# A two-layer transformer block on one core: the memory gemms and the last input projections are moved into the attention mixer, and the softmax rows are scaled on GpSimd

## The reference, cut to what matters

```python
for l in range(DEPTH):
    h = rmsnorm(x, norm_mix[l])
    proj = h @ w_in[l]
    ua, cq, ckv, kr, qc, kc, vc, ud = jnp.split(proj, IN_SPLITS, axis=-1)
    ya = conformer_conv(ua, ...)      # gate, 31-tap depthwise convolution, layernorm, silu, 256x256
    yb = mla(cq, ckv, kr, ...)        # 4 heads: softmax(q k' * 96**-0.5 + mask) v
    yc = diff_attention(qc, kc, vc, positions, rel_bias, ...)   # softmax(a) - lam * softmax(b), heads of 32
    yd = multiscale_pool(ud, ...)     # windows of 2, 4, 8, 16 tokens
    x = x + jnp.concatenate([ya, yb, yc, yd], axis=-1) @ w_out[l]
    x = x + memory_cross_attention(rmsnorm(x, norm_xa[l]), mem, mem_norm[l],
                                   xa_wq[l], xa_wk[l], xa_wv[l], xa_wo[l])
    x = x + conv_glu_ffn(rmsnorm(x, norm_ffn[l]), ffn_up[l], ffn_dw[l], ffn_dw_b[l], ffn_down[l])
return rmsnorm(x, norm_final)
```

## Time and profile before

| | us |
|---|---|
| median of 3 runs (1737.64 to 1742.45) | 1741.35 |
| the profiled execution, its own time | 1740.95 |
| its span, first to last instruction | 1739.2 |
| TensorE busy in the span | 1626.3 |
| VectorE busy | 1104.0 |
| ScalarE busy | 706.7 |
| GpSimd busy | 235.1 |

### The profile page before, as it was taken

The page is one execution under the profiler, slowest core; times in us unless marked ns, Lnnn a source line. Parts: engine busy times, 40 slices in busy tenths (PEclk is TensorE's granted clock), DMA queues, the critical chain, the costliest instruction groups (busy, mean ns, idle before and its releaser), DMA issues. The chain is left out here.

```text
span 1739.2 us, 22473 instructions
## 1 busy us (share of the span) xinstructions
PE 1626.3 (94%) x7664; PEld 1279.8 (74%) x7664; DVE 1104.0 (63%) x1604; ACT 706.7 (41%) x1082; POOL 235.1 (14%) x212
## 2 busy tenths in 40 slices
PE   6889989889999999999998999988999999999996
PEld 3567687668767888888876768657867788888874
DVE  8967974775445764764764886485444674575575
ACT  3232345763334432432442335674243442342343
POOL 5510511112012000000020150112102000000002
PEclk9889999999999999999998999999999999999998
DMA  3143133322212233323224224241211333332323
GB/s 135 47 155 97 61 121 98 103 67 89 81 36 86 97 95 93 96 94 95 94 86 134 83 73 132 78 129 52 94 49 63 95 97 96 97 96 90 99 80 109
DMA packets 50048, 159.69 MB, mean 92 GB/s; under 512 B 6576, under 2 KB 6832, under 8 KB 49072
## 3 DMA queue, kind: packets, MB, share of 16 engines
q1 hardware_dynamic: 49968, 158.63, 29.4%
HBM read 144.97 MB, written 7.34 MB: 88 GB/s over the span
## 5 line engine op out<-in xcount | busy, mean ns | idle before, releaser
L675 ACT ACTIVATE wh<-raw 128x1024 fp32r<-128x1024 f32 x246 | 260.9, 1061 | 657.5 <-PE psum L1235 646.3
L1233 PE MATMUL psum<-a_hi,wh 128*128 128x512 f32 x1072 | 423.1, 395 | 7.8 <-DVE wl L927 7.2
L927 DVE TENSOR_TENSOR wl<-raw,wh 128x1024 fp32r<-128x1024 f32 x246 | 302.7, 1231 | 189.6 <-ACT wh L675 189.4
L1234 PE MATMUL psum<-a_lo,wh 128*128 128x512 f32 x1072 | 419.6, 391 | 0.0
L1235 PE MATMUL psum<-a_hi,wl 128*128 128x512 f32 x1072 | 419.1, 391 | 0.0
L1233 PE MATMUL psum<-b_hi,wh 128*128 128x512 f32 x608 | 239.7, 394 | 5.6 <-DVE wl L927 2.5
L1233 PEld LDWEIGHTS psum<-a_hi,wh 128*128 128x128 f32 x1072 | 202.6, 189 | 56.8 <-DVE wl L927 12.2
L1234 PE MATMUL psum<-b_lo,wh 128*128 128x512 f32 x608 | 236.7, 389 | 0.0
L1235 PE MATMUL psum<-b_hi,wl 128*128 128x512 f32 x608 | 236.7, 389 | 0.0
L1234 PEld LDWEIGHTS psum<-a_lo,wh 128*128 128x128 f32 x1072 | 202.8, 189 | 43.1 <-issue 1.4
L1235 PEld LDWEIGHTS psum<-a_hi,wl 128*128 128x128 f32 x1072 | 202.7, 189 | 42.7
(11 more groups left out here) (209 smaller groups left out, 2145.3 us busy)
## 6 DMA issues: line engine op xcount, KB each, us to landing
raw<-in_w_main SPq DMA_DIRECT2D x106, 512.0 KB, 3.5
raw<-in_w_up SPq DMA_DIRECT2D x88, 512.0 KB, 3.5
raw<-in_w_down SPq DMA_DIRECT2D x32, 512.0 KB, 3.5
bias<-bias_scratch SPq DMA_DIRECT2D x32, 256.0 KB, 2.9
terms<-qk SPq DMA_DIRECT2D x48, 128.0 KB, 2.5
raw<-in_w_last SPq DMA_DIRECT2D x16, 384.0 KB, 3.0
bias_scratch<-stage SPq DMA_DIRECT2D x64, 64.0 KB, 1.6
raw<-in_w_first SPq DMA_DIRECT2D x6, 512.0 KB, 3.6
```

The lines of the kernel that those rows point to most:

```text
L675: act.activation(wh[:, b].rearrange("p k m -> p (k m)")[:, 0:width], raw[:, b, 0:width], ACT.Copy).then_inc(w_hi, 1)
L927: dve.tensor_tensor(wl[:, b].rearrange("p k m -> p (k m)"), raw[:, b, :], wh[:, b].rearrange("p k m -> p (k m)").bitcast(F32), ALU.subtrac ...
L1233: pe.matmul(out_ap, wh[:, b, k, :], his[:, k, :], start=(begin and i == 0), stop=False)
L1234: pe.matmul(out_ap, wh[:, b, k, :], los[:, k, :], start=False, stop=False)
```

## The change

- Projections 11 to 14, the eight memory key gemms and the eight memory value gemms now lie in the mixer: 11 to 14 at t 0 to 3, 15 to 22 at t 5 to 12, 23 to 30 at t 16, 18, 20, 22, 24, 27, 30 and 33 (CHUNK_AT), each at the end of its step on all engines. The mixer of TensorE has 38 steps, and VectorE has a 39th.
- The tiles are turned three steps behind their score (TURN_LAG) and not two. GpSimd multiplies the tile of 128 x 512 in place by the reciprocal sums, and `turn` is four transposes with the identity.
- The differential scores are plain float32 products over 32 rows of q and k, one for each map, at row offsets 0 and 32 (or 64 and 96) of the array; `terms`, its DMAs, the ScalarE copies and the GpSimd subtractions of the fp32r parts are gone. Both products wait until VectorE has read both banks of the step before. Their tiles lie in a ring of their own, `dring`, of four pairs.
- Turned tiles go to a ring of four (`ptr`). The splitting of the memory and the transposes of the differential values are at t 4.
- Taps: 4 in each of t 0 to 3, 3 in each of t 5 to 10, 2 behind each q head. The pooling windows are cut in two parts each that lie behind the tiles 3 to 6 in GpSimd's queue. Small products, layer norm, Silu and the order of the output tiles are moved to other steps. All bias loads but those of the first four are laid between the weight loads 27 to 33.

```diff
+CHUNK_AT = {**{t: 11 + t for t in range(4)}, **{t: 10 + t for t in range(5, 13)},
+            **{t: N_WV + i for i, t in enumerate((16, 18, 20, 22, 24, 27, 30, 33))}}
+TURN_LAG = 3
+STEPS = 38
...
@@ gpsimd
                     for u in range(32):
-                        if u >= 4:
-                            pool.wait_ge(t_full, u - 3)
-                        m = u if u < 16 else 2 * u - 16
-                        pool.wait_ge(rec_in, u + 1)
-                        pool.tensor_scalar(diag[:, u % 4, :], ident, rec[:, m:m + 1], None, ALU.mult).then_inc(diag_in, 1)
+                        if u < 16:
+                            pool.wait_ge(rec_in, u + 1)
+                            e, m = ering[:, u % RING, :], u
+                        else:
+                            pool.wait_ge(p_ready, u - 16 + 1)
+                            e, m = dring[:, 2 * u % 8, :], 2 * u - 16
+                        pool.tensor_scalar(e, e, rec[:, m:m + 1], None, ALU.mult).then_inc(scaled_in, 1)
+                        if u in (3, 5):
+                            window_sums(u // 2 - 1)
+                        if u in (4, 6):
+                            window_differences(u // 2 - 2)
...
@@ scalar, at the step's end
+                        if t == 4:
+                            act.wait_ge(memf_in, 16)
+                            act.wait_ge(g_full, N_WK)
+                            for k in range(KT):
+                                act.activation(memh[:, k, :], memf[:, k, :], ACT.Copy,
+                                               scale=v("g_mem", k)).then_inc(m_hi, 1)
+                            for i in range(2):
+                                act.activation(vc[:, :, P * i:P * i + P],
+                                               v_wait(f"vc{i}").rearrange("p (t f) -> p t f", t=4),
+                                               ACT.Copy).then_inc(v_act, 1)
...
+                        n = CHUNK_AT.get(t)
+                        if n is not None:
+                            hi(n + 2)
+                        if n is not None and n >= N_WK:
+                            act.wait_ge(g_full, n + 1)
...
@@ vector
+                        if t < 4:
+                            convolve(4)
+                        elif t > 4:
+                            convolve(3)
...
+                        n = CHUNK_AT.get(t)
+                        if n is not None:
+                            if n < N_WK:
+                                scaled(n, places[n])
+                            lo(n + 2)
...
@@ tensor
-                    for t in range(36):
+                    for t in range(STEPS):
...
                             h, qb, _ = tile_at(t - 16)
-                            if qb == 0:
-                                pe.wait_ge(terms_in[h % 3], (h // 3 + 1) * 6 * 16)
+                            if t == 16:
+                                pe.wait_ge(g_dve, 11)
+                            bank_seen(2 * t - 15)
                             for m in range(2):
-                                k = 2 * t - 16 + m
-                                bank_seen(k)
-                                pe.matmul(SC[k % 2], terms[h % 3][0:96, m, qb * P:qb * P + P],
-                                          terms[h % 3][0:96, 2 + m, :], start=True, stop=True).then_inc(s_full, 1)
-                        if t < 8:
-                            n = N_WV + t
-                            gemm(n, n % 2, memh, meml, M, "act")
+                                rows = slice(64 * (h % 2) + 32 * m, 64 * (h % 2) + 32 * m + 32)
+                                pe.matmul(SC[m], qk[rows, h // 2, qb * P:qb * P + P], qk[rows, 2 + h // 2, :],
+                                          start=True, stop=True).then_inc(s_full, 1)
...
+                        if t >= 5 and t % 2 == 1 and t <= 35:
+                            weighted_pair((t - 5) // 2)
+                        n = CHUNK_AT.get(t)
+                        if n is not None:
+                            if n < N_WK:
+                                gemm(n, n % 2, a_hi, a_lo, free="in")
+                            else:
+                                gemm(n, n % 2, memh, meml, M, "in" if n < N_WK + 2 else "act",
+                                     ready=(lambda i: pe.wait_ge(m_lo, i + 1)) if n == N_WK else None)
```

More of the change, by code:

```diff
@@ L991, in latents @@
                             dve.tensor_tensor(cq[64:P, 1, :], cq[64:P, 1, :], rope[64:P, :], ALU.mult).then_inc(kr_in, 1)
-                    for n in range(15):
+                    for n in range(11):
                         if n == 0:
@@ L1274, in _ @@
                     product("stat_kv", (ones, ssum[:]))
-                    gemms(10, 4, a_hi, a_lo, S, "in")
-                    gemm(14, 0, a_hi, a_lo, free="in")
+                    gemm(9, 1, a_hi, a_lo, free="in")
+                    gemm(10, 0, a_hi, a_lo, free="in")
                     pe.wait_ge(kr_in, 1)
@@ L1294, in _ @@
                         last.then_inc(v_full, 1)
-                    for i in range(2):
-                        ps = bank(f"vc{i}")
-                        for kb in range(4):
-                            last = pe.transpose(ps[:, P * kb:P * kb + P], vct[:, i, kb * P:kb * P + P], ident)
-                        last.then_inc(v_full, 1)
-                    gemm(15, 1, memh, meml, M, "in", ready=lambda i: pe.wait_ge(m_lo, i + 1))
-                    gemm(16, 0, memh, meml, M, "in")
-                    gemms(N_WK, KT, memh, meml, M, "act", lead=2)
                     def bank_seen(m):
@@ L1318, in turn @@
                         for kb in range(4):
-                            last = pe.matmul(TR[u % 2][:, P * kb:P * kb + P], e[:, P * kb:P * kb + P], diag[:, u % 4, :],
-                                             start=True, stop=True)
+                            last = pe.transpose(TR[u % 2][:, P * kb:P * kb + P], e[:, P * kb:P * kb + P], ident)
                         last.then_inc(t_full, 1)
@@ new lines, in _ @@
+                                pe.matmul(SC[m], qk[rows, h // 2, qb * P:qb * P + P], qk[rows, 2 + h // 2, :],
+                                          start=True, stop=True).then_inc(s_full, 1)
+                        if TURN_LAG <= t < 32 + TURN_LAG:
+                            turn(t - TURN_LAG)
+                        if t == 4:
+                            pe.wait_ge(g_dve, 13)
+                            for i in range(2):
+                                ps = bank(f"vc{i}")
+                                for kb in range(4):
+                                    last = pe.transpose(ps[:, P * kb:P * kb + P], vct[:, i, kb * P:kb * P + P], ident)
+                                last.then_inc(v_full, 1)
@@ new lines, in _ @@
+                        if t in (8, 12):
+                            i = t // 4 - 2
+                            pe.wait_ge(ud_done, 2 * i + 2)
+                            product(f"pool{i}", (sw[:, SW_POOL + P * i:SW_POOL + P * i + P], ud[:, i, PPAD:]))
+                        if t == 10:
+                            pe.wait_ge(acc_done, 2)
+                            product("ln_mean", (ones, acc[:, 0, :]), (ones, acc[:, 1, :]))
+                        if t == 14:
+                            pe.wait_ge(cent_sq, 2)
+                            product("ln_var", (ones, sqx[:, 0, :]), (ones, sqx[:, 1, :]))
```

340 lines of the change are left out of this document (151 added, 189 removed).

## The result

The changed kernel took 1768.86 us (median of four runs, 1765.85 to 1772.81) against 1739.69 before (median of four; the 1741.35 given above is that of the first three): ratio 1.0168, 95% interval 1.0137 to 1.0199. The forecast of 1731 had the wrong sign, and its range ended at 1757. The profiled execution took 1772.81 us with a span of 1770.8, 31.6 more than before, at a mean granted clock of 0.960 (0.977 before).

What follows compares the result with a forecast made beforehand. TensorE, busy 94% of the span, was taken as the bound; stage terms -21.8 + 1.5 - 28 + 17 + 28 - 1.3 gave -4.6 us a layer, -9.2 in two, so 1731 us, range 1709 to 1757.

Steps and rivals of the forecast that it cites:

- Projections and key gemms: First layer: four gemms leave the projections, -21.8 us; the memory key gemms move into the mixer, -28 us.
- A pair: Two float32 differential score products at different array rows take three of four passes, 1.3 us, against 0.5 to 0.6 before.
- Scaling on GpSimd: Scaling a 128 x 512 tile in place takes 2.0 us (bounds 1.6 to 2.6); 32 of them are no bound.
- Rival E: GpSimd is late: a scaling costs 3.3 us and VectorE's taps slow beside it; +9 us a layer, 1750; chance 0.13.
- Small products: Stage after the projections: transposes leave, but q heads wait behind VectorE's taps; +1.5 us a layer in all.
- t 4 and 5: Mixer steps where splitting the memory and copies hold up the first product with the values: 13.2 us.
- t 10: Mixer step where tile 7's turn waits about 4 us for GpSimd behind the pooling windows: 9.8 us in all.
- From t 16: Mixer's second half: lo delays the minima in VectorE's queue, two steps take 8.4 us; stage +28 us a layer.
- Tail: Last stage of a layer: three output tiles done earlier, one v product and root late; -1.3 us.
- stages 4 and 5: The mixer's t 0 to 15 (+17 us) and t 16 to the last product with the values (+28 us).
- the forecast's check by work: TensorE's own work unchanged within 1 or 2 us; its waiting falls from some 40 to some 33 us a layer.
- Rival D: Clock falls from t 13 onward, since transposes do not count as busy; +8 us a layer, 1757; chance 0.12.

Runs made afterwards that it cites:

- e5_heads: Changed kernel with VectorE's convolution taps dealt out anew, more behind input chunks and fewer ahead of the q heads: 1766.0 us, ratio 1.0149.
- e1_windows: Changed kernel with GpSimd's two pooling windows cut in pieces so that tile 7 is scaled before its turn is due: 1775.6 us, ratio 1.0183.
- e3_lo_late: Changed kernel with VectorE, from step 16 on, making a chunk's lower part behind the following step's minima instead of before them: 1751.9 us, ratio 1.0082.
- e11_heads_second: Changed kernel with e5_heads' taps, lower parts at the following step's end from step 16, and ScalarE's step-20 copies ahead of the Silu: 1728.4 us, ratio 0.9939.
- e9_all: e11_heads_second plus cut windows, mean product at step 11, v copies first at step 4, earlier inverse sum, more taps behind last q head: 1707.8 us, ratio 0.9813.

## Why the prediction was wrong, step by step

- **Projections and key gemms** (-21.8, -28): right, -21.6 and -27.4. **t 0 to 3** (25.9): right, 25.8.
- **A pair** (1.3, from three passes of four): wrong, 1.06. By the Trainium skill (TensorE: Matmul & The Clock Gate, part 3, 3.07 times for four row tiles) the estimate was near 1.0, and the 1.06 bears it out. The sum was 0.25 us a pair on the safe side, so by itself it would have made the kernel faster than forecast.
- **Scaling on GpSimd** (2.0): right. It took 1.57 to 2.41, the slow ones beside VectorE's taps. Rival E's 3.3 was not seen; the slower taps that it named were, see t 10.
- **Small products** (+1.5): +4.7. The four late taps and the wait were named; that the wait costs the clock behind it was not. Of the 6.7 us over e5_heads, 1.8 are the wait and 4.8 are the clock: eight records take 6.98 instead of 4.30 us, and the eight of the keys (`kn`) 5.90 instead of the 3.75 of e5_heads.
- **t 4 and 5** (13.2): 14.3 and 15.6. The wait for the copies was forecast, the half clock behind it not.
- **t 10** (9.8, a wait of 4 for GpSimd): 14.1 and 14.9. This step failed in its reading too. VectorE's taps were priced at 0.77 us, though the forecast's own rows had them at 1.05 beside the windows (rival E); three took 3.79, and a lower part 2.20 where 1.22 is usual. The product for the mean was also laid right behind three taps of its own step. So VectorE was as late as GpSimd, and to help GpSimd alone gave nothing (e1_windows). How much of VectorE's lateness is slow taps and how much the order was not tried apart.
- **From t 16** (+28; two steps in 8.4): the mechanism, lo ahead of the minima, was right, and e3_lo_late measured it at 1.1 us a gemm step. Where the clock fell the steps were wrong: t 28 to 30 took 17.3 and 14.7 us where 13.5 was forecast, and t 17 to 24, forecast at 39.8, took 39.8 in the first layer but 43.3 in the second, whose step 22 was slow.
- **Tail** (-1.3): +1.4 and +3.1; not looked into by a run.

The step of the forecast that failed is the one that adds up waits at their length: "each of the waits in stages 4 and 5 is a sum of latencies that may be 10% off". It failed twice. Behind new waits of 1.5 to 5 us TensorE often worked at half clock, which the sum put at nothing. And there was more waiting than it had: the forecast's check by work let TensorE's waiting fall from some 40 to some 33 us a layer, but over the span its idle time rose by 12 us a layer. The rows above show it at t 10, where VectorE was late as well as GpSimd, and at steps 21 and 22. Rival D said the clock would fall and gave 1757, the nearest number, but for transposes and with 0.12; its own mark, a grant under 0.87, was not reached (0.92 and 0.89 from t 16). The Trainium skill's sentence on transposes (same page, part 4), on which D leaned, does not decide the time of this mixer: e11_heads_second has the turns as transposes too, among its other products, and a clock of 1.00 from t 16 on. The Trainium skill (same page, part 1, "HAM oscillation — how this bites in real kernels") tells of a kernel whose TensorE is throttled again at each wait for data. The rows here agree in kind, with waits for semaphores, but not at each wait: behind the 2.00 us ahead of the pair of step 22 in the first layer the clock stayed at 1.00.

So the loss is shown to come from the order in the queues, not from the added work as such: with the same 7472 matmul records and the same scalings, e9_all is 61 us faster than the changed kernel by the medians. Between the two profiled executions it is 64.5 us of span. TensorE's busy time has 29.3 of them (1633.8 to 1604.5), which with the same matmuls is the clock's part, and its idle time has the other 35.2 (137.0 to 101.8). How many of the waits were themselves made longer by slow stretches before them is not separated.

## What to carry to other kernels

Where a change lays big matmuls over a latency chain, write down each wait that it makes on TensorE and what stands behind it; a wait can cost its length and a stretch at half clock behind it. When a wait names one engine, look at the next wait too: two engines may be late together, and only helping both shows. Do small moves within the other engines' queues (what the matmul engine needs first, taps and table loads last) before judging a pipelining change: this one is -1.9% or +1.7% by them and the place of one product. And matmuls without use, put into a wait to keep the clock up, test the clock alone only while they are shorter than the wait.

## What was not expected of the hardware

- The same wait does not always cost the same. At step 20 the changed kernel waits 1.5 us ahead of the pair in both layers; in the first the gemm behind it takes 3.7 us, in windows with a clock of 0.71 to 0.86, in the second 3.05 at 1.00. With e5_heads, step 22 was slow in the first layer and steps 20 and 30 in the second, where they had not been. So an edit ahead of the mixer went with 6.3 us more from t 16 on in one layer and 2.7 in the other, in stages that it does not touch.
- VectorE beside GpSimd: 1.26 us a tap (three in 3.79) instead of 0.77, and 2.20 instead of 1.22 for a lower part, while GpSimd worked without a pause from 244 to 256 us. Both read two tensors in SBUF. The Trainium skill (GPSIMD Engine Reference, the table of part 1) names such instructions as those that contend with GpSimd, and the rows agree.
